# Twelve expert weight units of a two-layer trunk loaded one row of each block of eight at a time

## What is computed

```
def swiglu(h, w_gate, w_up, w_down):
    return (jax.nn.silu(h @ w_gate) * (h @ w_up)) @ w_down

def moe_swiglu(h, router, w_gate, w_up, w_down):
    logits = (t @ router).astype(jnp.float32)
    top_v, top_i = lax.top_k(logits, TOP_K)
    w = jax.nn.softmax(top_v, axis=-1)
    combine = jnp.sum(jax.nn.one_hot(top_i, N_EXPERTS, dtype=jnp.float32) * w[..., None], axis=1)
    for e in range(N_EXPERTS):
        out = out + combine[:, e:e + 1] * swiglu(t, w_gate[e], w_up[e], w_down[e])
```

## Time and profile before

| | |
|---|---|
| median of three runs | 1328.41 us |
| the profiled execution | 1327.61 us |
| its span, first to last instruction | 1325.8 us |
| TensorE busy | 1267.3 us (96%) |
| VectorE, ScalarE, GpSimd busy | 363.1, 284.5, 30.9 us |
| moved by the DMA engines | 435.54 MB, mean 329 GB/s |

### The profile page before, as it was taken

The page is one execution under the profiler, slowest core; times in us unless marked ns, Lnnn a source line. Parts: engine busy times, 40 slices in busy tenths (PEclk is TensorE's granted clock), DMA queues, the critical chain, the costliest instruction groups (busy, mean ns, idle before and its releaser), DMA issues.

```text
span 1325.8 us, 27799 instructions
## 1 busy us (share of the span) xinstructions
PE 1267.3 (96%) x12897; PEld 764.0 (58%) x12897; DVE 363.1 (27%) x470; ACT 284.5 (21%) x357; POOL 30.9 (2%) x34
## 2 busy tenths in 40 slices
PE   7999999999999999999999999899989799989886
PEld 6978888888888884333644444444444254344354
DVE  5976444444664353003100200100200100030010
ACT  5855444333546531000000000000000000000000
POOL 2000000000230000000000000000000000000000
PEclk9999999999999999999999999999999999999999
DMA  9546555555442199999999999999999999999994
GB/s 332 181 164 225 184 189 190 191 189 160 159 128 65 43 421 393 383 426 426 424 426 425 426 424 425 426 426 425 425 425 424 426 425 425 426 425 426 425 425 188
DMA packets 70324, 435.54 MB, mean 329 GB/s; under 512 B 4656, under 2 KB 6816, under 8 KB 45632
## 3 DMA queue, kind: packets, MB, share of 16 engines
q1 hardware_dynamic: 69744, 433.10, 81.5%
q0 software_dynamic: 368, 0.63, 0.1%
q10 hardware_dynamic: 96, 0.03, 0.0%
HBM read 432.69 MB, written 1.05 MB: 327 GB/s over the span
## 4 chain that ended last, share of the span: by engine, by line
PE 78%; DMA 18%; ACT 2%; DVE 1%; issue 0%; SPq 0%; POOL 0%; DVEq 0%
PE ps L1272 27%; PE ps L1289 14%; DMA ring<-in_moe_w_down_dram 14%; PE ps L848 9%; PE ps L850 9%; PE ps L849 9%; DMA ring<-in_moe_w_gate_dram 4%; PE ps L1238 1%; PE ps L1078 1%; PE ps L1105 1%; PE ps L864 1%; PE ps L890 1%; PE ps L877 1%; PE ps L880 1%; PE ps L879 1%
## 5 line engine op out<-in xcount | busy, mean ns | idle before, releaser
L1272 PE MATMUL ps<-ring,xg 128*32 128x512 f32 (+1 forms) x4384 | 421.5, 540 | 21.1 <-DMA ring<-in_moe_w_up_dram 13.7
L1272 PEld LDWEIGHTS ps<-ring,xg 128*32 128x32 f32 x4384 | 140.7, 110 | 292.4 <-issue 254.0
L1457 DVE TENSOR_TENSOR wlo<-raw,whi 128x2048 fp32r<-128x2048 f32 x73 | 166.5, 2288 | 74.2 <-PE ps L850 72.2
L547 ACT ACTIVATE whi<-raw 128x2048 fp32r<-128x2048 f32 x73 | 139.2, 1915 | 85.3 <-PE ps L850 83.8
L848 PE MATMUL ps<-whi,hT_hi 128*128 128x512 f32 x384 | 153.3, 399 | 2.4 <-DVE wlo L1457 1.4
L850 PE MATMUL ps<-whi,hT_lo 128*128 128x512 f32 x384 | 149.8, 390 | 0.0
L849 PE MATMUL ps<-wlo,hT_hi 128*128 128x512 f32 x384 | 149.5, 389 | 0.0
L1289 PE MATMUL ps<-ring,aTL 128*32 128x256 f32 x2352 | 133.4, 380 | 6.0 <-DMA ring<-in_moe_w_down_dram 5.8
L1937 DVE TENSOR_TENSOR gtL<-gtL,ps 128x896 f32<-128x896 f32 x12 | 13.1, 1088 | 404.2 <-PE ps L1272 404.2
L1289 PEld LDWEIGHTS ps<-ring,aTL 128*32 128x32 f32 x2352 | 77.2, 110 | 58.2 <-DMA ring<-in_moe_w_down_dram 7.2
L1289 PE MATMUL ps<-ring,aTS 128*32 128x256 f32 x1568 | 90.0, 380 | 9.5 <-DMA ring<-in_moe_w_down_dram 8.6
(11 more groups left out here) (292 smaller groups left out, 1011.8 us busy)
## 6 DMA issues: line engine op xcount, KB each, us to landing
ring<-in_moe_w_gate_dram SPq DMA_DIRECT2D x56, 1792.0 KB, 22.9
ring<-in_moe_w_down_dram SPq DMA_DIRECT2D x56, 1792.0 KB, 28.6
ring<-in_moe_w_up_dram SPq DMA_DIRECT2D x54, 1792.0 KB, 24.5
raw<-in_fox_w_in_dram SPq DMA_DIRECT2D x16, 1024.0 KB, 5.5
raw<-in_ffn_w_gate_dram SPq DMA_DIRECT2D x14, 1024.0 KB, 5.2
raw<-in_ffn_w_up_dram SPq DMA_DIRECT2D x14, 1024.0 KB, 5.1
raw<-in_ffn_w_down_dram SPq DMA_DIRECT2D x14, 1024.0 KB, 5.1
ring_last<-in_moe_w_up_dram SPq DMA_DIRECT2D x8, 1792.0 KB, 26.4
```

Source lines behind the costliest of these rows:

```text
L547: nc.scalar.activation(whi[:, m % HR], raw[:, DENSE[m]], ACT.Copy).then_inc(hi_done, 1)
L1272: ins = mm(ps[strip(c), 2 * a + b, 0:width], x, w[:, c * STRIP + first:c * STRIP + first + width], start=n == 0, stop=n == KT - 1, skip_gr ...
L1457: nc.vector.tensor_tensor(wlo[:, m % LR], raw[:, DENSE[m]], whi[:, m % HR].bitcast(F32), ALU.subtract).then_inc(lo_done, 1)
```

## The change

Positions 0, 12, 24 and 36 of UNITS, which is four units of each of the three later pairs (12 of the 192), are loaded in nine transfers in place of one. Call partitions 0 to 7, 8 to 15 and so on the blocks of eight. The first transfer takes row 0 of each of the 16 blocks and raises `arrived`. The next six take rows 1 to 6 of each block, 16 partitions each. The last row of each block (row 7) goes in two transfers of eight partitions, one over the blocks of partitions 0 to 63 and one over the blocks of 64 to 127. These eight later transfers raise one new semaphore, `rest_in`, and PE waits for it too before it reads such a unit. The bytes that are moved, and where they go, stay as they were.

```
+UNEVEN = range(0, PAIR_UNITS, 12)
+BLOCK = 8
...
+    def uneven(self, i):
+        return self.table is UNITS and i in UNEVEN
+
+    def rest(self, i):
+        return at(16 * BLOCK * (len(UNEVEN) * (self.ahead - 1) + UNEVEN.index(i) + 1), 16 * BLOCK * len(UNEVEN), self.i)
...
-                sp.dma_start(dst, src).then_inc(arrived[group.slot(i)], 16)
+                if not group.uneven(i):
+                    sp.dma_start(dst, src).then_inc(arrived[group.slot(i)], 16)
+                    return
+                sp.dma_start(dst[0:P:BLOCK], src[0:P:BLOCK]).then_inc(arrived[group.slot(i)], 16)
+                for r in range(1, BLOCK - 1):
+                    sp.dma_start(dst[r:P:BLOCK], src[r:P:BLOCK]).then_inc(rest_in, 16)
+                for p in (0, P // 2):
+                    last = slice(p + BLOCK - 1, p + P // 2, BLOCK)
+                    sp.dma_start(dst[last], src[last]).then_inc(rest_in, 16)
...
                 pe.wait_ge(arrived[group.slot(i)], group.landed(i))
+                if group.uneven(i):
+                    pe.wait_ge(rest_in, group.rest(i))
```

More of the change, by code:

```diff
@@ L355, in hybrid_trunk @@
         out_done, sumsq_v, par_in2, ff_T = sem("out_done"), sem("sumsq_v"), sem("par_in2"), sem("ff_T")
+        rest_in = sem("rest_in")
         h_f_done, xn_act = sem("h_f_done"), sem("xn_act")
```

## The result

The changed kernel takes 1482.0 us (median of 4 runs, 1477.5 to 1487.2) against 1328.45 us of the kernel before on the same chip: ratio 1.116, interval 1.1141 to 1.1179. That is 154 us more, or 12.8 us for each of the twelve changed units, and outside my range, which ended at 1374. The profiled execution took 1481.7 us with a span of 1479.9.

The account below looks back on a forecast made before the run. The prediction took the DMA engines' loading of weights as the bound, half of the engines ending late. Its terms, -6.5 + 0.4 = -6.1 us, gave 1322.3 us on the median's scale, with a range from 1319.5 to 1374 us.

Parts of the forecast that it names:

- speed of a row in the split form: DMA writes of the changed units into SBUF: between 0 and 51.7 us lost, taken as nothing.
- half of the paths: Rival, chance 0.29: changed units' rows reach only half the ways into SBUF, 8.6 us per unit, 1374 us, softened 1348.
- Shift of load: DMA engines: short transfers move 6.5 us of rows from the late half of the engines to the early half, a gain.
- The gap of 14 us: End of the weight loads: eight engines finish about 14 us late; instruction loading, 10 us on each, inferred as most of it.
- Completions: DMA engines of the late half: six more completions per changed unit cost 0 to 1.6 us, taken as 0.4 us.
- SP's issues: SP's queue: nine issues take 3.3 us per changed unit in place of 0.37, covered by queued units, cost nothing.
- TensorE's waits: TensorE: twelve more semaphore waits, 0.5 us in all beside 35.5 us of idle time, cost nothing.
- The split mechanism: Rival, chance 0.29: in changed units, rows written through half the ways into SBUF run at half rate, 1345 to 1380 us.

Follow-up runs that it names:

- e1: Against the kernel before, the twelve units in eight transfers of every eighth partition, 16 rows each, without the short transfers: 1461.5 us, ratio 1.100.
- e7: Against the kernel before, the twelve units in four transfers of 32 partitions, every fourth one: 1327.7 us, ratio 0.9997.
- e12: Against the kernel before, the twelve units in four transfers of 32 neighbouring partitions: 1482.3 us, ratio 1.116.
- e13: Against the kernel before, the twelve units in two transfers of every other partition, 64 rows each: 1328.3 us, ratio 1.000.
- e9: Against the kernel before, the twelve units in two transfers, the lower 64 partitions and the upper 64: 1473.2 us, ratio 1.109.
- e14: Against the kernel before, the first four units of each later pair, side by side, in two transfers by halves of the partitions: 1398.6 us, ratio 1.0531.
- e5: Against the kernel before, the nine-transfer form for the first unit of each later pair alone, three units in all: 1359.7 us, ratio 1.0237.
- e8: Against the kernel before, three units, one of each later pair, in 16 transfers of eight partitions, four apart: 1364.8 us, ratio 1.0279.
- e2: Against the kernel before, the twelve units in eight transfers of all 128 partitions, an eighth of the columns each: 1332.7 us, ratio 1.0038.
- e3: Against the kernel before, the twelve units in eight transfers of 16 neighbouring partitions, 16 whole rows each: 1477.9 us, ratio 1.113.

## Why the prediction was wrong

**The step that failed is "speed of a row in the split form".** Between 0 and 51.7 us I took the lower end, "because engine by engine the row size and the number of rows stay what they are in the nearest row, the whole unit". That is true of each engine alone and says nothing of two engines that write at the same time. The rows of whole units, at an even 425 GB/s, say nothing of it either, since there every engine seems to have its own places. The nearest row by size was the farthest by the property that decides. Measured, a row took 1.22 us in place of 0.54 in the first dip, and the term that I put at nothing is 134 of the 154 us (e1). e7 against e12, and e13 against e9, show that the places that a transfer reaches make the difference, with the number of transfers, rows and packets alike.

**The rival "half of the paths" had the mechanism and a price of a third.** Its full price was 51.7 us and its softened one half of that; measured are 154. I counted one unit at half rate, 4.3 us, and thought that engines which are apart would soften it. The opposite holds. By e9 and e14 some 6 to 8 us go with each change from whole to split and back, and 4.3 with the unit itself. The chains of e12 show how: an engine that is ahead in its changed unit and one that still writes a whole unit are both slow, and later the other way round. That the cost grows with the distance between the engines is shown by e5's three dips, of 6.7, 9.6 and 12.9 us; no run changed that distance alone, so this part rests on the two growing together.

**"Shift of load"** was right in the count: 71,088 - 69,744 = 1344 packets, 112 for each unit, are 7 x 16 + 2 x 8 - 16 completions, so an eight-row transfer does use eight engines. The direction failed. The two short transfers use the same eight engines, as I had it, but these are not one of the halves: around the first changed unit of the changed kernel, two of the eight chains with nine rows also carry instruction packets, as late engines do, and six of the other eight. So most of the late engines are relieved and about two are loaded, and the time goes by the last engine: 12 rows more on it are 6.5 us lost, not won. A view of e8 fits this, where the short transfers put 24 rows more on eight engines; from 1344 us on two engines alone (2 x 26.9 GB/s) still carry:

```profile
1344.00:1348.00 4.00, 3.40 (x64) 1.84 (x60) 0.00 (x0) 0.00 (x0) 0.00 (x0) 1.00 0.13 54
```

But e1, whose shares are even, ends with two engines alone as well:

```profile
1440.00:1444.00 4.00, 2.56 (x48) 1.30 (x44) 0.00 (x0) 0.00 (x0) 0.00 (x0) 1.00 0.13 54
```

So the tail is not the short transfers' alone, and what makes up the rest of the 20 us between e1 and the changed kernel stays open; that short transfers reach still fewer ways would fit too.

The gap of 14 us itself fits instruction loading by place and by size, as I had inferred. In the chains of the kernel before, 64 of the 72 instruction packets from 600 us on are on the eight engines that end last (63 of 72 in e13). Such a packet takes 1.07 us, and the row behind it 1.03 us in place of 0.54, so nine of them make some 14 us, where I had counted 10.

**"Completions"** cost nothing that can be seen: e7 has 48 more per unit and e13 16, and both are at the time of the kernel before.

**"SP's issues"** were put at half of what they take, 3.3 against 6.3 us, because the rows of before had no strided transfer of 16 rows. They were named as a point at which the prediction would fail, and did not decide: with e2's longest issue at 7.0 us that kernel loses 5 us in all. **"TensorE's waits"**, nothing, was right: the same waits are in e7 and e13.

**The chances.** The split mechanism had 0.29, with the evenness of whole units for it; the spread of the engines, which I held against it, was what made it dear. The range ended at the rival's price for the ideal case. What was missing was an upper bound on the unknown that wasn't built on the same idealisation.

## What to carry to other kernels

In a stretch bound by DMA, split a load so that each piece still reaches all groups of partitions, by columns, by every second or by every fourth partition; not by blocks of neighbouring partitions or by every eighth one, which cost 10 to 13 us for each 1.8 MB here. Read GB/s beside the DMA share: in these runs a share of 1.0 with half the rate meant that engines held each other up, and no count of bytes or transfers will find it. When a disturbance hits engines that are out of step, price it by how far they are apart as well as by its own length: here 6.7, 9.6 and 12.9 us for the same unit.

## What the runs showed of the hardware

- A load of 1.8 MB in two transfers by halves of the partitions costs 12.1 us among whole ones (e9), where half rate alone would add 4.3, and 5.9 us where four stand side by side (e14).
- The same load in two transfers of every other partition, or in four of every fourth, costs nothing (e13 1328.3 us, e7 1327.7).
- Transfers of 16 neighbouring partitions (e3) lost 12.5 us per unit, and of 16 partitions eight apart (e1) 11.2.
- Instruction packets of 16 KB fall on eight of the 16 engines (64 of 72 in the kernel before), take 1.07 us each and slow the row behind them to 1.03 us, so that those eight end 14.5 us after the others.
- An issue of SP for 16 rows eight partitions apart takes 0.50 us and for eight such rows 0.62, against 0.33 for a whole unit.
- A copy of eight rows of 14,336 bytes within HBM is dealt over 16 engines in 32 packets, while a load of eight rows into SBUF adds 16 packets on eight engines.
